# Eight modulation parts moved among the input projections, three output banks, and an earlier feed at the start of a two-block transformer kernel

## The reference, cut to what matters

```
# block 1
x = x + 0.5 * swiglu(rms_norm(x, norm_ffn1), ffn1_gate, ffn1_up, ffn1_down)
p = rms_norm(x, norm_mix) @ w_in               # 13 column blocks of 256
sb_q, sb_k, sb_v, rw_in = split(p)
o_sb = stick_breaking_attention(q, k, v)
o_rw = rwkv7_time_mix(rw_in, ...)              # token shift, LoRAs, chunked recurrence
x = x + concat(o_sb, o_rw) @ w_out
x = x + 0.5 * swiglu(rms_norm(x, norm_ffn2), ffn2_gate, ffn2_up, ffn2_down)
# block 2
sh1, sc1, g1, sh2, sc2, g2 = split(silu(c) @ w_mod + b_mod, 6)      # the modulation
csh1, csc1, ... = split(silu(c_ctx) @ w_mod + b_mod, 6)
h = rmsnorm(x) * (1 + sc1) + sh1               # attention, Fourier branch, gates
x = x + g1 * mix ; x = x + g2 * hier_moe(...)  # 16 experts
return rmsnorm(x, final_g)
```

## Time and profile before

| | us |
|---|---|
| median of 3 runs (range) | 1144.02 (1143.0 to 1149.3) |
| the profiled execution's own time | 1144.87 |
| its span in the trace | 1143.1 |
| PE busy in the span | 1106.3 (97%) |
| DVE, ACT, POOL busy | 600.7, 449.2, 25.0 |
| DMA, mean over the span | 223 GB/s |

### The profile page before, as it was taken

One profiled execution on the slowest core, in us unless ns is written; L12 is line 12 of the kernel. 1 busy time (PEld: TensorE's weight loads), 2 busy tenths in 40 slices (PEclk: granted clock), 3 DMA queues, 4 the chain that ended last, 5 costly groups with the idle time before them and its releaser, 6 DMA issues.

```text
span 1143.1 us, 20468 instructions
## 1 busy us (share of the span) xinstructions
PE 1106.3 (97%) x8832; PEld 905.4 (79%) x8832; DVE 600.7 (53%) x803; ACT 449.2 (39%) x572; POOL 25.0 (2%) x30
## 2 busy tenths in 40 slices
PE   6999999899998999999999999999999999999996
PEld 6999998899877757999999999988889753434342
DVE  5545546689644185645555475177748652222122
ACT  6333334764431125433334333266674530111112
POOL 0000000000212010000000000000000000000000
PEclk9999999999999999999999999999999999999999
DMA  9655556454475854555655144243257889999994
GB/s 342 215 189 190 191 191 189 133 180 149 156 296 177 300 188 143 184 185 183 187 185 189 65 149 147 77 145 112 79 183 258 343 334 400 421 412 418 422 418 175
DMA packets 121001, 254.36 MB, mean 223 GB/s; under 512 B 6226, under 2 KB 91490, under 8 KB 109411
## 3 DMA queue, kind: packets, MB, share of 16 engines
q1 hardware_dynamic: 119730, 248.61, 61.1%
q10 hardware_dynamic: 1200, 4.71, 1.2%
HBM read 252.25 MB, written 1.06 MB: 222 GB/s over the span
## 4 chain that ended last, share of the span: by engine, by line
PE 88%; DVE 5%; ACT 3%; DMA 3%; issue 1%; SPq 1%; ACTq 0%; DVEq 0%
PE ps L736 56%; PE ps L715 30%; DMA arena<-in_w_exp_up 2%; ACT arena L1446 2%; DMA ring<-in_ffn_gate 1%; DVE ring_r L2094 1%; PE ps L1194 1%; DVE arena L2146 1%; ACT L1446 0%; SPq L582 0%; PE ps L724 0%; DVE arena L2161 0%; PE ps L1397 0%; PE ps L908 0%; ACT arena_r L1446 0%
## 5 line engine op out<-in xcount | busy, mean ns | idle before, releaser
L736 PE MATMUL ps<-hall_r,arena_r 128*128 128x256 f32 x1760 | 324.5, 283 | 4.7 <-DVE hall_r L1999 4.7
L1993 DVE TENSOR_TENSOR ring_r<-ring,arena_r 128x2048 fp32r<-128x2048 f32 x89 | 203.6, 2290 | 172.2 <-ACT arena_r L1446 170.1
L736 PE MATMUL ps<-arena_r 128*128 128x256 f32 (+1 forms) x1216 | 284.4, 324 | 1.2 <-DVE arena_r L2385 1.2
L736 PEld LDWEIGHTS ps<-hall_r,arena_r 128*128 128x128 f32 x1760 | 274.5, 189 | 6.7 <-issue 3.0
L1446 ACT ACTIVATE arena_r<-ring 128x2048 fp32r<-128x2048 f32 x100 | 190.9, 1915 | 163.9 <-PE ps L736 154.0
L736 PE MATMUL ps<-hall_r,ring_r 128*128 128x256 f32 x880 | 246.7, 280 | 0.0
L736 PEld LDWEIGHTS ps<-arena_r 128*128 128x128 f32 x1216 | 202.8, 188 | 19.6 <-DVE arena_r L2385 1.4
L1446 ACT ACTIVATE arena<-ps 128x512 f32<-128x512 f32 (+3 forms) x133 | 77.9, 599 | 329.1 <-PE ps L736 188.9
L715 PE MATMUL ps<-arena 64*64 64x32 f32 (+8 forms) x2264 | 199.6, 308 | 6.2 <-issue 2.8
L715 PEld LDWEIGHTS ps<-arena 128*64 128x64 f32 (+3 forms) x2264 | 121.2, 143 | 70.2 <-issue 61.7
L736 PEld LDWEIGHTS ps<-hall_r,ring_r 128*128 128x128 f32 x880 | 168.2, 191 | 0.8
(11 more groups left out here) (254 smaller groups left out, 1038.4 us busy)
## 6 DMA issues: line engine op xcount, KB each, us to landing
ring<-in_w_in SPq DMA_DIRECT2D x35, 1024.0 KB, 5.2
arena<-in_w_exp_down SPq DMA_DIRECT2D x32, 1024.0 KB, 12.3
ring<-in_w_mod SPq DMA_DIRECT2D x24, 1024.0 KB, 5.5
ring<-in_ffn_gate SPq DMA_DIRECT2D x22, 1024.0 KB, 5.3
ring<-in_ffn_up SPq DMA_DIRECT2D x22, 1024.0 KB, 5.4
ring<-in_ffn_down SPq DMA_DIRECT2D x22, 1024.0 KB, 5.0
arena<-in_w_exp_up SPq DMA_DIRECT2D x16, 1024.0 KB, 15.0
ring<-in_w_exp_gate SPq DMA_DIRECT2D x16, 1024.0 KB, 12.1
```

What stands on the lines that cost most here:

```text
L736: m = pe.matmul(out_, w[i], h[j], start=start and i + j == 0, stop=stop and j == 1, skip_group_check=group)
L1993: tt(lo(n), slot(n), hi(n), ALU.subtract).then_inc(S("w_lo"), 1)
```

## The change

It does seven things.

1. **Order of the pieces.** The 13 w_in pieces and modulation parts 0 to 7 are numbered together (`mixed_order`). Part 0 runs before the transposes of the second norm, part 1 after project(1), 2 after (3), 3 after (4), 4 after (6), 5 after (7), 6 after (9), 7 after (10). The later parts move forward: parts 8 to 15 stand where 0 to 7 stood, and none is left after inverse level 0.
2. **Banks.** Projections use three banks (j % 3) and wait for copy_out(j-3) and shift(j-3); bank 3 collects modulation parts 0 to 7, kept in a tile of its own (`mod_first`).
3. **Norms by bank.** `turn_apart` puts the transposed tiles k = 0 to 3 in banks of their own (4, 5, 6, 7) and 4 to 7 in banks 1 and 2, so that ACT and DVE can take them singly. It serves norms n1, n2 and n3.
4. **`outward`.** The first product behind each of these norms runs over k on the outside and both column halves inside.
5. **Zeros.** PE multiplies zeros eight times at the start and twice after the first transposes.
6. **Start.** Piece 0 is loaded and split in two halves by k; the small constants come before the vectors; the large constants table moves to SP's queue, behind the first three chunks.
7. **LoRA weights** are loaded by ACT's queue before the second norm, not in the middle of it.

```diff
+        mixed_order = "m0 w0 w1 m1 w2 w3 m2 w4 m3 w5 w6 m4 w7 m5 w8 w9 m6 w10 m7 w11 w12".split()
+        def n_win(j):
+            return N_WIN + mixed_order.index(f"w{j}")
+        def n_mod(i):
+            return N_WIN + mixed_order.index(f"m{i}") if i < 8 else N_WMOD + i
...
+        def turned_at(k):
+            return ps[:, (4, 5, 6, 7, 1, 1, 2, 2)[k], T * (k in (5, 7)):T * (k in (5, 7)) + T]
...
+            sp.dma_start(cols(N_FFN1)[:, 0:KT // 2, :], w_cols["ffn1_gate"][:, 0:KT // 2, 0:256]).then_inc(
+                S("first_in"), 16)
...
                 for i in range(FFN_PEEL):
                     chunk(i)
+                if n0 == N_FFN1:
+                    sp.dma_start(cst[:, early:], a["consts"][:, early:]).then_inc(S("consts"), 16)
...
+            def outward(tag, bank, w_hi_, w_lo_, by, low_half=None):
+                for k0 in range(0, KT, by):
+                    ks = range(k0, k0 + by)
...
+                    for k in ks:
+                        pe.wait_ge(*W(tag + "_hi", k + 1))
+                        for f in range(2):
+                            mm(out_(f), f_of(w_hi_, k, f), h_hi[:, k, :], start=k == 0 and f == 0, stop=False, group=True)
+                    if low_half is not None:
+                        pe.wait_ge(*low_half[k0 // by])
+                    for k in ks:
+                        for f in range(2):
+                            mm(out_(f), f_of(w_lo_, k, f), h_hi[:, k, :], start=False, stop=False, group=True)
+                    for k in ks:
+                        pe.wait_ge(*W(tag + "_lo", k + 1))
...
+            pe.wait_ge(*W("c_zero", 2))
+            zeros = c_pad[:, :, :].rearrange("p k n -> p (k n)")
+            for i in range(8):
+                mm(ps[:, 0, 0:256], zeros[:, 0:P], zeros)
             pe.wait_ge(*W("ident_in", 16))
-            norm_transposes("n1", 4)
+            turn_apart("n1")
+            for i in range(2):
+                m = mm(ps[:, 0, 0:256], zeros[:, 0:P], zeros)
...
             pe.wait_ge(*W("consts", 16))
-            norm_transposes("n2", 4)
+            mod_part(0)
+            turn_apart("n2")
...
-                if j >= 4:
-                    pe.wait_ge(*W("win_copied", j - 3))
-                if 4 <= j < 11:
-                    pe.wait_ge(*W("shifted", j - 3))
+                if j >= 3:
+                    pe.wait_ge(*W("win_copied", j - 2))
+                if 3 <= j < 10:
+                    pe.wait_ge(*W("shifted", j - 2))
...
             project(0)
             project(1)
+            mod_part(1)
             pe.wait_ge(*W("small_w", 48))
             pe.wait_ge(*W("x1_done", 4))
             pe.wait_ge(*W("tanh_w", 1))
...
             four(4, lambda o, k: mm(o, head_mean, sq[:, k, :]), "sbo_ms")
-            mod_part(8)
-            mod_part(9)
             pe.wait_ge(*W("sbo_root", 1))
             for level in range(1, 6):
                 if level > 1:
                     for t in range(TT):
                         inv(level, t, "x")
-                    for i in ((10, 11), (12,), (13,), (14, 15))[level - 2]:
-                        mod_part(i)
...
-            norm_transposes("n3", 4)
             pe.wait_ge(*W("mod_cols", 3))
             pe.wait_ge(*W("y_root", 1))
+            turn_apart("n3")
...
             high_in(0)
             high_in(1)
-            fetch(ACT.Sqrt)
-            norm("n2")
-
             act.dma_start(small_w["w2"][0:64, :], a["rw_w2"]).then_inc(S("small_w"), 16)
             act.dma_start(small_w["a2"][64:128, :], a["rw_a2"]).then_inc(S("small_w"), 16)
             act.dma_start(small_w["g2"], a["rw_g2"]).then_inc(S("small_w"), 16)
+            fetch(ACT.Sqrt)
+            norm("n2")
+
             norm_cols_hi("n2", lambda k: V("norm_mix", k))
```

More of the change, by code:

```diff
@@ L553, in _, with load_mod @@
                 sp.dma_start(x[:, t, :], a["x"][t * P:(t + 1) * P, :]).then_inc(S(f"x_in{t}"), 16)
+            sp.dma_start(cols(N_FFN1)[:, 0:KT // 2, :], w_cols["ffn1_gate"][:, 0:KT // 2, 0:256]).then_inc(
+                S("first_in"), 16)
             ffn(N_FFN1, "ffn1")
[L555 to L557 removed]
+            def load_mod(i):
                 vec_, part = divmod(i, 4)
[L559 removed]
+                load(n_mod(i), w_cols["w_mod_2"][:, 2 * part:2 * part + 2, vec_ * D:(vec_ + 1) * D])
+            win_cols = [6 + c for c in RW_ORDER] + list(range(6))
+            for what in mixed_order:
+                i = int(what[1:])
+                if what[0] == "m":
+                    load_mod(i)
+                else:
+                    load(n_win(i), c256("w_in", win_cols[i]))
+            for i in range(8, 24):
+                load_mod(i)
             for c in range(4):
@@ L1009, in _ @@
                 sb_scores(p)
-            for i in range(4):
+            for i in range(8, 12):
                 mod_part(i)
@@ L1510, in _ @@
             norm("n1")
-            split(N_FFN1)
-            act.dma_start(cst[:, early:], a["consts"][:, early:]).then_inc(S("consts"), 16)
-            act.wait_ge(*W("vec_in", 16))
-            norm_cols_hi("n1", lambda k: V("norm_ffn1", k))
+            for g in range(2):
+                act.wait_ge(*(W(f"w_in_slot{N_FFN1 % RING}", 16) if g else W("first_in", 16)))
+                f(hi_cols(N_FFN1)[:, 4 * g:4 * g + 4, :], cols(N_FFN1)[:, 4 * g:4 * g + 4, :], ACT.Copy).then_inc(
+                    S("w_hi" if g else "first_hi"), 1)
+                act.wait_ge(*W("vec_in", 16))
+                norm_cols_hi("n1", lambda k: V("norm_ffn1", k), range(4 * g, 4 * g + 4))
             split(N_FFN1 + 1)
@@ L1576, in copy_out, with keep_mod @@
                 f(o, bank, ACT.Copy).then_inc(S("win_copied"), 1)
+            def keep_mod(b):
+                act.wait_ge(*W("w_used", n_mod(8 * b + 7) + 1))
+                kept = mod_rows[:, 512 * b:512 * (b + 1)] if b else mod_first[:, :]
+                f(kept, ps[:, (3, 6, 7)[b], :], ACT.Copy).then_inc(S("mod_kept"), 1)
             copy_out(0)
@@ L1637, in _ @@
                 f(b_tok[:, t, :], ps[:, 4 + t, :], ACT.Copy).then_inc(S("b_tok"), 1)
+            keep_mod(0)
             copy_out(11)
@@ L1664, in sb_weights @@
                     f(part, part, ACT.Exp).then_inc(S("sb_att"), 1)
-            def keep_mod(b):
-                act.wait_ge(*W("w_used", N_WMOD + 8 * (b + 1)))
-                f(mod_rows[:, 512 * b:512 * (b + 1)], ps[:, 6 + b % 2, :], ACT.Copy).then_inc(S("mod_kept"), 1)
             act.wait_ge(*W("sb_z", 2))
```

169 lines of the change are left out of this document (108 added, 61 removed).

## The result

The changed kernel takes 1154.61 us (median of 4 runs, 1152.28 to 1155.68), the kernel before 1144.49 us beside it (4 runs). The ratio is 1.0078, with a 95% interval of 1.0048 to 1.0107: 10 us slower, where 1144.1 was forecast and 1151.0 was the upper end. The profiled execution, the slowest of the four, has a span of 1153.9 (before: 1143.1).

The account below looks back on a forecast made before the run. PE, busy 97% of the span, was taken as the bound. Gains and losses summed to +0.1 us against the profiled execution (1144.87), 0.85 above the 1144.02 median, giving 1144.1; range 1138 to 1151.

Parts of the forecast that it names:

- Wait 1: Before lora_w: PE waits for tanh, behind ACT's split of late-loaded w_in piece 5; loss 10.4 us, bounds 8.5 to 11.5.
- wait 2: At project(8): late w_in piece 8 delays kk_norm and shift(5), for which PE waits; loss 1.9 us (0 to 4).
- Start: First weight piece: half the bytes needed first, so PE ends piece 0 at 16.0, not 21.0; gain 5.0 us.
- second norm: LoRA loads gone from ACT there and tiles taken singly, so PE starts earlier and projections run faster; gain 1.6 us.
- the stage ahead of level 1: Before the inverse levels: two parts go, but PE waits for ACT's root, which comes 0.6 earlier; gain 0.6 us.
- the term of half clock: Behind the lora_w wait: PE works at half clock for a while; loss 1.8 us, between 0.8 and 3.4.
- the parts: Seven modulation parts among the projections, 0.95 us each: loss 6.65 us, with 1.1 back at q_ms.
- "issue" gap: Inverse levels: 2.82 us idle, read as PE's code arriving late, goes with its half clock; gain 3.8 us, low end 0.
- The gap stays: Rival: a 2.8 us idle stretch with half clock still appears, at the levels or elsewhere; 1147.9 us, chance 0.15.
- the waits are short: Rival: w_in pieces 5 and 8 land 4.8 us after issue; 9.3 us lost, not 14.1; 1139.3 us, chance 0.16.
- The ring starves ACT more: Rival: later loads and dearer clock at piece 5 and 8 splits; 18.7 us, not 14.1; chance 0.17.
- The zeros don't hold the clock: Rival: at the start PE idles again before the first product and falls to half clock; 1145.8 us, chance 0.07.

Follow-up runs that it names:

- tanh-first profile: Changed kernel with ACT's split of w_in piece 5 moved from ahead of tanh to behind the LoRA sigmoids; 1147.05 us, ratio 1.0007.
- PE fed in both waits: Changed kernel plus matmuls into unused banks while PE waits: 26 ahead of lora_w, 11 ahead of project(8); 1152.04 us, ratio 1.0055.
- the move undone: Changed kernel with piece order, modulation parts' places and four banks as before; start, norms by bank and early LoRA loads kept; 1140.25 us, ratio 0.9944.
- With piece 8 moved as well: Changed kernel with piece 5's split behind the LoRA sigmoids and piece 8's splits behind kk_norm (ACT) and k_bar (DVE); 1140.73 us, ratio 0.9949.

## Why the prediction was wrong

**The structure was right.** The two waits came at the two places, by the chain that was laid out. Wait 1 was 11.0 us for 10.4 (bounds 8.5 to 11.5), wait 2 2.9 for 1.9. The loads landed 7.15 and 8.17 us after issue. The forecast had 6.5, in which the modulation piece asked for 1 us earlier was already counted; why it was more, the runs don't show. Start, second norm, third norm and the stage ahead of level 1 came within 0.3 us.

**The step that failed is the clock.** It is the term of half clock in the sum: 1.8 us, behind the first wait alone, bounds 0.8 to 3.4, and nothing anywhere else. Read are 4.4 behind the first wait and 1.6 behind the second; in the levels 28.86 us against 25.8 at full clock (tanh-first profile), 3.1; at the recurrence 1.5. That is 10.6 us, 8.8 more than the forecast's term, out of a miss of 10.7 in the span. The waits themselves, 0.6 and 1.0 too small, and the parts, 0.85, are most of the rest. The first two terms of the clock are the move's; the 4.6 in the levels and the recurrence seem to come and go with the execution, as with PE fed in both waits. The profile is of the slowest of the four, with a mean granted clock of 0.984; the fastest took 1152.28 us at 0.989, and is still above 1151.0. Two errors are in the first two terms. The size was taken from one stretch behind an idle of 2.8 us in the earlier trace rows, where the matmuls are narrow and little was lost; behind lora_w stand the dense ones, 5.63 us for 2.96. And it was charged once, though the sum held a second wait of 1.9 us; the runs with PE fed show that each of the two brings its own loss, and that none is left in the projections when both are filled. As for the levels, the stretch of half clock was taken as a consequence of the gap that went. It is not: it comes without the gap too, in some executions.

**The levels.** The parts and the "issue" gap went as forecast: at full clock the stage takes 25.8 us for 37.45, less by 11.7 (forecast 11.0). The gap is in all four traces with six parts between the levels (2.82 before; 2.40, 2.94 and 2.65 with the move undone, with three banks and without the zeros), and no trace with two or no parts has one over 0.2. What it is, late code or not, these runs don't show.

**The rivals.** "The gap stays" and "the waits are short" did not happen. "The ring starves ACT more" is what happened, its two numbers being later loads and a dearer clock; it was given 0.17 and reached up to 1152.5 only with the gap staying. With the gap gone it ends at 1148.7, so even this case stayed below the result: its clock (3.4) was again charged once. "The zeros don't hold the clock" would have cost 1.7; the run without zeros shows 0.9 at the most. The Trainium skill ("DMA: Bandwidth & Descriptors", section on the anatomy of one DMA), from which the prediction worked out 4.4 us for a load of 1 MB, fits its formula to loads issued by GpSimd. These are SP's; their median is 5.2, and the two that mattered took 7.15 and 8.17.

**What was missed outside the sum.** The forecast worked with the waits as they would be, not as they could be avoided. Piece 5 was split at 213.6 us in the kernel before, and project(5) began after 241. So its split did not have to stand ahead of the tanh. That the price was the order on ACT, which the move had made late, would have shown in the same layout of the four streams.

## What to carry to other kernels

When a change puts pieces into a shared ring, list for every piece which use now releases its load, and look on the splitting engine for a short operation behind each piece that comes later than before: move the split behind it, and every split ahead of it that was covered until then. Price each wait of TensorE with the wait itself and several microseconds of half clock behind it, in dense matmuls, once for every such wait: 3.7 us of idling cost as much clock as 11.0, and 1.9 as much as 2.9. (The wait of 1.43 us with three banks alone cost none.) A short piece of work is free only where the engine waits; taking it from there brings the wait back, with its clock.

## What the runs showed of the hardware

- After 3.7 us and after 11.0 us of idling PE ran at 0.50 for about the same time (8.4 and 9.3 us; 216.6 to 225.0 and 223.7 to 233.0) and the 16 LoRA matmuls took 5.62 and 5.63 us for 2.96 at full clock. With piece 8 moved as well, PE idled 3.39 us and the half clock lasted to 226.5, 10 us.
- Matmuls that compute nothing, issued while PE waits, kept the clock at 1.00: 2.96 us for the same 16 after a fed wait of 12.35.
- Eight runs of one kernel lay in two groups 4.7 us apart, three at a mean granted clock of 0.995 to 0.997 and five at 0.991 to 0.993. The profiled one, of the slower group, loses 4.6 us in a stage of small matmuls and behind it that run partly at half clock.
- The first transposes take 3.47 us after an idle start and 2.19 to 2.24 behind zeros, while the granted clock reads 1.00 in both: here that column doesn't account for the difference.
- Two weight loads of 1 MB, each issued 1 us behind another, landed 7.2 and 8.2 us after issue; the median over the kernel is 5.2.
